# Multi-scale pooling moved out of the projection on GpSimd and into the output projection on VectorE, tile by tile

## The chip, the cores and the metric

The kernel runs on one core of a Trainium2 chip. A core has a matrix engine (TensorE, PE in the profile), a vector engine (VectorE, DVE), an engine for activations (ScalarE, ACT), a general engine (GpSimd, POOL) and one that mostly issues transfers (SyncE, SP). Each works through its instructions in the order in which they are written, and waits on semaphores where another engine or a transfer has to be done first. Transfers between the main memory (HBM) and the core's own memory (SBUF) run on 16 DMA engines. PE writes its results into PSUM, which VectorE and ScalarE read. The metric is the device time of one execution in microseconds.

## What is computed

One encoder layer over two groups of tokens, 1024 and 2048 long, with shared weights of width 1024. The half of it that matters here is the mixer: a projection of the normed input gives attention latents and 512 pooling channels `u`; attention and pooling are joined and go through one output projection.

```python
POOL_WINDOWS = (2, 4, 8, 16)          # one per group of 128 channels
def multiscale_pool(u, w_pool, pool_scale):
    ...
    for g, w in enumerate(POOL_WINDOWS):
        lo = jnp.clip(t - w // 2, 0, s)
        hi = jnp.clip(t + (w - w // 2), 0, s)
        ...
        means.append((cs_g[:, hi] - cs_g[:, lo]) / count)
    d = (mean - ug.astype(jnp.float32)).astype(u.dtype)
    y = jnp.einsum('bsgc,gcd->bsgd', d, w_pool).reshape(b, s, D_POOL)
    return y * pool_scale

def encoder_layer(...):
    h = rmsnorm(x) * (1 + sc1) + sh1
    c_q, c_kv, k_pe, u = jnp.split(h @ w_in, ...)
    att = latent_attention(c_q, c_kv, k_pe, ...)
    pool = multiscale_pool(u, w_pool, pool_scale)
    x = x + g1 * (jnp.concatenate([att, pool], axis=-1) @ w_out)
    h = rmsnorm(x) * (1 + sc2) + sh2
    return x + g2 * expert_choice_ffn(h, ...)
```

So each token's pooled value is the mean of `u` over a window of 2, 4, 8 or 16 tokens around it, cut at the ends of its group, minus `u` itself. The weights `w_pool` and `pool_scale` are folded into the output weights by the attention stage and play no part below.

## The kernel before

Six stages follow one another, each with a block of its own: `in_proj` (to about 430 us), `latent_proj` (to 645), `attention` for either group (to 1655), `out_proj` (to 1985), `selection` and `experts`. Results between stages lie in HBM scratch tensors with names in `s_`. Products are made of three passes of fp32r halves (`..h` high, `..l` low), so every operand is split: ScalarE writes the high half, VectorE subtracts it for the low half.

**`in_proj`** works on 24 tiles of 128 tokens in pairs and stores, among others, the pooling channels as `s_ut`, 4 groups of 128 channels by 3072 tokens, and the latents as `s_ct`.

**`latent_proj`** goes over 6 blocks of 512 tokens. A block is a list ORDER of 16 PSUM results: keys, queries, values and the rotary pairs r and t. PE makes them, ScalarE and VectorE split them (L955, L1009; rotary L990, L996, L947, L999), SP stores them (L872). Into this list, four times a block, the 24 jobs of the pooling are set: a job is one group of 128 channels over 512 tokens. SP loads it with 8 tokens on either side (`fetch`, L830), GpSimd doubles the window by adding a row to itself shifted (L794, the last step L792) and does the ends of a group with their own counts (L800, L803), VectorE scales and subtracts `u` (`difference`, L969), SP stores it to `s_diff` (`store_diff`, L837). The places are numbers in ORDER (POINTS), the same on SP and VectorE; two buffers `prj_u` and `prj_diff` alternate. SP's queue is one line: a job's store waits in front of the stores of the block's other results.

**`out_proj`** goes over 12 blocks of two tiles u = 0, 1. For block r:

- SP loads `mix[:, u]`, its lower half from `s_att` (L1628) and its upper half from `s_diff` (L1633), and the softmax denominators `rden` (L1631); then the residual input `x` (L1641), which for tile u waits until the previous block's `x1` of that tile is added. Since the queue is one line, the loads of `mix` for block r + 1 stand behind the `x` load for tile 1 of block r, and so behind the addition of `x1` for tile 1 of block r - 1.
- GpSimd multiplies the attention half by `rden` (`scale`, L1652) and adds `x1 = gated + x` (L1662). Its order is scale(r, 1), x1(r, 0), scale(r + 1, 0), x1(r, 1).
- ScalarE writes the high half of `mix` (`mix_high`, L1726), VectorE the low half (`mix_low`, L1800).
- PE multiplies (L1703 to L1705), behind tile 0 it transposes the previous block's `xn` (L1679), behind tile 1 it makes the router's logits (L1690).
- VectorE multiplies the result by the gate (`gated`, L1779); ScalarE squares `x1` for the norm (L1749, L1756), VectorE scales it to `xn` (L1787, L1793), and ScalarE's queue stores `x1` and `xn` (L1754, L1731).

VectorE's order in a block is the hand-written one that the change touches:

```python
def body(r, g, before, last=False):
    mix_low(r, 1, before is None)
    for u in range(2):
        dve.wait_ge(o_ready, 2 * r + u + 1)
        ...  # gated[:, u]
        if u == 0:
            if not last:
                mix_low(r + 1, 0, False)
    ...  # logits, reciprocal, xn
```

Blocks 0, 1, 4 and 11 are written out, 2 and 3 and 5 to 10 run in loops.

Of the kernel before, what the change touches and what calls it, by code (L numbers as in the profile page):

```python
# [30 lines left out]
P = 128  # L31
# [21 lines left out]
QUADS, QUAD = 4, 32  # L53

# [45 lines left out]
def in_proj(nc, w, keep):  # L100
# [17 lines left out]
    with ExitStack() as ctx:  # L118
# [25 lines left out]
        eps = m.sb("eps", [P, 1])  # L144
        t_ps = [m.ps(f"t_ps{i}") for i in range(2)]
# [19 lines left out]
        eps_set = m.sem("eps_set")  # L165
        x_squared = m.sem("x_squared")
# [37 lines left out]
        def _(sp):  # L204
# [38 lines left out]
            sp.dma_start(rope[:], w["k_rope"].rearrange("t p a c -> p t a c")).then_inc(rope_loaded, 16)  # L243
            for n in range(TILES):
# [8 lines left out]
                sp.dma_start(w["s_ut"][n % TB * UG:(n % TB + 1) * UG, :, b * T:(b + 1) * T].rearrange("g p t -> p g t"),  # L253
# [6 lines left out]
            sp.wait_ge(gates_stored, 64)  # L260
            for i in range(2):
# [384 lines left out]
def latent_proj(nc, w, keep):  # L646
# [10 lines left out]
    PAD = max(WINDOWS) // 2  # L657
    SPAN = BANK
    JOBS = [(g, c, o) for g in (1, 0) for c in range(len(WINDOWS)) for o in range(0, SEQS[g], SPAN)]
# [6 lines left out]
    JOBS_PER = len(JOBS) // NB  # L666
    POINTS = [PER * (i + 1) // JOBS_PER - 2 for i in range(JOBS_PER)]
    SIMPLE = [i for i, (kind, _) in enumerate(ORDER) if kind in "kqv"]
    SLOT = {"q": 0, "r": NQ, "k": NQ + RT, "v": NQ + RT + KT}
    with ExitStack() as ctx:  # L670
# [14 lines left out]
        u = m.sb("u", [P, 2, SPAN + 2 * PAD])  # L685
        sums = m.sb("sums", [P, 2, SPAN + 2 * PAD])
        diff = m.sb("diff", [P, 2, SPAN])
        edge = m.sb("edge", [P, len(WINDOWS), 2 * PAD])
        ends = m.sb("ends", [P, 2 * PAD])
# [16 lines left out]
        edge_in = m.sem("edge_in")  # L706
# [3 lines left out]
        total_ready = m.sem("total_ready")  # L710
        ends_ready = m.sem("ends_ready")
        pads_set = m.sem("pads_set")
        u_in = [m.sem(f"u_in{i}") for i in range(2)]
        summed = m.sem("summed")
        diff_ready = m.sem("diff_ready")
        diff_stored = [m.sem(f"diff_stored{i}") for i in range(2)]
        block = ctx.enter_context(nc.Block())

        def ends_of(n):
            g, _, o = JOBS[n]  # L720
            return o == 0, o + SPAN == SEQS[g]
# [39 lines left out]
        def _(pool):  # L761
            m.clear_last(pool)
            step = sequence(summed)
            pads = sequence(pads_set)

            def set_pads(n):

# [8 lines left out]
            for n in range(2):  # L776
                set_pads(n)
# [1834 lines left out]
```

## Time and profile before

| | us |
|---|---|
| median of three runs | 3834.94 |
| lowest and highest | 3832.25, 3835.29 |
| the profiled execution, device time | 3837.06 |
| its span in the trace | 3835.3 |
| PE busy | 3552.2 (93%) |
| DVE busy | 2026.7 (53%) |
| ACT busy | 1879.4 (49%) |
| POOL busy | 1271.3 (33%) |
| mean DMA rate | 141 GB/s |

The busy shares are sums over all stages, and stages have different limits. A stage is read from a window over it (busy time of each engine, granted clock of TensorE as a share of its full 2.4 GHz, share of the DMA engines) and from the timeline of single engines, where a row gives the start, the duration, what it does, and in brackets how long the engine sat idle before and what ended that wait. Starts are microseconds from the start of the span.

### The profile page before, as it was taken

The page shows a single profiled execution, that of the slowest core. Times are in us where ns is not written, and L with a number is a line of the kernel's source. Part 1 is how long each engine was busy: PE and PEld are TensorE (multiplying, and loading weights), DVE is VectorE, ACT ScalarE, POOL GpSimd, SP SyncE. Part 2 cuts the span into 40 slices and gives each one's busy share as a digit, 9 for nine tenths or more (in the row PEclk, how much of TensorE's full clock was granted, in tenths as well). Part 3 has the DMA queues.
Part 4 walks back from the last instruction along what each step waited for, and adds up shares of the span by engine and source line. Part 5 has one row for each costly group of instructions (what it writes and reads, how often), then busy time and mean ns, then how long its engine had stood idle before and what let it go on. Part 6 is the DMA issues. An engine that isn't in the chain of part 4 may idle for free. (4 is left out here: it accounts for less than half of the span.)

```text
span 3835.3 us, 54529 instructions
## 1 busy us (share of the span) xinstructions
PE 3552.2 (93%) x19090; PEld 3085.7 (80%) x19090; DVE 2026.7 (53%) x3177; ACT 1879.4 (49%) x3261; POOL 1271.3 (33%) x1006
## 2 busy tenths in 40 slices
PE   8999798998999999979973999999999999999993
PEld 5999676676777777757762999999999999999992
DVE  3333345787888888822237644444444444444444
ACT  4444223886889899933320343444434344343433
POOL 1111045886999899932320000000000000000000
PEclk8999898998999999989985999999999999999996
DMA  7445699630222222046641445445454444545447
GB/s 245 159 159 94 207 378 330 117 76 21 56 51 45 46 45 50 11 131 195 194 149 44 133 145 163 153 153 162 144 164 143 146 140 150 164 143 164 152 122 279
DMA packets 368694, 539.12 MB, mean 141 GB/s; under 512 B 39618, under 2 KB 257010, under 8 KB 365566
## 3 DMA queue, kind: packets, MB, share of 16 engines
q1 hardware_dynamic: 340356, 448.80, 38.4%
q0 software_dynamic: 13824, 50.34, 5.4%
q10 hardware_dynamic: 14336, 37.77, 2.5%
q8 instruction: 93, 1.52, 0.2%
q14 instruction: 85, 0.70, 0.1%
HBM read 394.27 MB, written 142.48 MB: 140 GB/s over the span
## 5 line engine op out<-in xcount | busy, mean ns | idle before, releaser
L1535 POOL TENSOR_TENSOR att_pr<-att_e,att_pr 128x512 fp32r<-128x512 f32 x640 | 815.8, 1299 | 138.8 <-ACT att_pr L1388 129.7
L2250 POOL DMA_INDIRECT s_x<-moe_ye,moe_to_add x48 | 92.9, 1935 | 1438.3 <-DVE moe_ye L2471 1429.1
L1453 DVE TENSOR_REDUCE att_mx<-att_m_ps 128x1 f32<-128x512 f32 x640 | 423.4, 682 | 68.7 <-PE att_m_ps L1266 60.6
L2409 DVE TENSOR_TENSOR keep_wl<-keep_raw,keep_wh 128x1024 fp32r<-128x1024 f32 x380 | 440.1, 1221 | 33.6 <-ACT keep_wh L2339 33.5
L2339 ACT ACTIVATE keep_wh<-keep_raw 128x1024 fp32r<-128x1024 f32 x380 | 370.0, 1045 | 123.1 <-PE moe_d_ps L2316 123.1
L1382 ACT ACTIVATE att_e<-att_s_ps 128x512 f32<-128x512 f32 x640 | 378.4, 591 | 67.8 <-PE att_s_ps L1293 36.8
L1388 ACT ACTIVATE att_pr<-att_e 128x512 fp32r<-128x512 f32 x640 | 402.7, 629 | 17.6 <-issue 2.2
L2366 ACT ACTIVATE moe_silu<-moe_a_ps 128x384 f32<-128x384 f32 x128 | 62.8, 491 | 653.3 <-PE moe_u_ps L2289 653.3
L1475 DVE TENSOR_TENSOR att_acc_ps<-att_acc_ps,att_e 128x512 f32<-128x512 f32 x544 | 374.9, 689 | 12.9 <-ACT att_e L1382 6.7
L2447 DVE TENSOR_TENSOR moe_hf<-moe_u_ps,moe_silu 128x384 f32<-128x384 f32 x128 | 71.4, 558 | 544.4 <-ACT moe_silu L2366 544.4
L2287 PE MATMUL moe_a_ps<-moe_xh,keep_wh 128*128 128x384 f32 x1024 | 345.7, 338 | 2.1 <-DVE moe_xl L2417 2.1
L2288 PE MATMUL moe_a_ps<-moe_xl,keep_wh 128*128 128x384 f32 x1024 | 345.1, 337 | 0.0
L2289 PE MATMUL moe_a_ps<-moe_xh,keep_wl 128*128 128x384 f32 x1024 | 344.9, 337 | 0.0
L2289 PE MATMUL moe_u_ps<-moe_xh,keep_wl 128*128 128x384 f32 x1024 | 344.4, 336 | 0.0
L2288 PE MATMUL moe_u_ps<-moe_xl,keep_wh 128*128 128x384 f32 x1024 | 344.2, 336 | 0.0
L2287 PE MATMUL moe_u_ps<-moe_xh,keep_wh 128*128 128x384 f32 x1024 | 344.2, 336 | 0.0
L1307 PE MATMUL att_o_ps<-att_pr,keep_ahead 128*128 128x512 f32 x1024 | 323.6, 397 | 2.5 <-POOL att_pr L1535 2.5
L2314 PE MATMUL moe_d_ps<-keep_wh,moe_hh 128*128 128x512 f32 x768 | 309.1, 402 | 4.9 <-DVE moe_ye L2471 3.0
L2316 PE MATMUL moe_d_ps<-keep_wh,moe_hl 128*128 128x512 f32 x768 | 302.8, 394 | 0.0
L2315 PE MATMUL moe_d_ps<-keep_wl,moe_hh 128*128 128x512 f32 x768 | 300.3, 391 | 0.0
L1307 PEld LDWEIGHTS att_o_ps<-att_pr,keep_ahead 128*128 128x128 f32 x1024 | 193.2, 190 | 48.8 <-POOL att_pr L1535 5.1
L1291 PE MATMUL att_s_ps<-keep_ahead 97*128 97x512 f32 x544 | 223.7, 411 | 4.0 <-issue 2.5
(284 smaller groups left out, 7702.1 us busy)
## 6 DMA issues: line engine op xcount, KB each, us to landing
keep_raw<-w_gate SPq DMA_DIRECT2D x64, 1024.0 KB, 5.1
keep_raw<-w_up SPq DMA_DIRECT2D x64, 1024.0 KB, 7.5
keep_raw<-w_down SPq DMA_DIRECT2D x64, 1024.0 KB, 6.7
inp_raw<-w_ada SPq DMA_DIRECT2D x48, 512.0 KB, 6.1
s_ct<-inp_ct SPq DMA_DIRECT2D x24, 640.0 KB, 3.1
prj_ct<-s_ct SPq DMA_DIRECT2D x6, 2560.0 KB, 12.5
s_kn<-prj_out SPq DMA_DIRECT2D x24, 512.0 KB, 9.1
s_qn<-prj_out SPq DMA_DIRECT2D x24, 512.0 KB, 9.2
```

Of the source, the lines that this page charges most:

```text
L1307: mm = nc.tensor.matmul(o_ps[b % 2][:, :], v[h][:, kt, :], pr[:, s % RING, a, :], start=(kt == 0 and a == 0), stop=(kt == NT - 1 and a == 1))
L1382: nc.scalar.activation(e[:, s % RING, :], s_ps[s % 2][:, :], ACT.Exp, scale=SCALE).then_inc(exp_done, 1)
L1388: nc.scalar.activation(pr[:, s % RING, 0, :], e[:, s % RING, :], ACT.Copy).then_inc(hi_done, 1)
L1453: nc.vector.tensor_reduce(mx[:, u % CB, u // CB:u // CB + 1], m_ps[u % MB][:, :], AX, ALU.max).then_inc(max_part, 1)
L1475: step = nc.vector.tensor_tensor(acc_ps[:, :], acc_ps[:, :], e[:, s % RING, :], ALU.add)
L1535: nc.gpsimd.tensor_tensor(pr[:, s % RING, 1, :], e[:, s % RING, :], pr[:, s % RING, 0, :].bitcast(F32), ALU.subtract).then_inc(lo_done, 1)
L2287: nc.tensor.matmul(out, hi, xh[:, k, :], start=(k == 0), stop=False)
L2288: nc.tensor.matmul(out, hi, xl[:, k, :], start=False, stop=False)
L2289: mm = nc.tensor.matmul(out, lo, xh[:, k, :], start=False, stop=(k == KD - 1))
L2314: nc.tensor.matmul(out, h_hi, wh[:, c % 2, k, :], start=(k == 0), stop=False)
L2339: nc.scalar.activation(wh[:, s, part, :], raw[:, s, part, :], ACT.Copy).then_inc(w_hi_done, 1)
L2409: nc.vector.tensor_tensor(wl[:, s, part, :], raw[:, s, part, :], wh[:, s, part, :].bitcast(F32), ALU.subtract).then_inc(w_lo_done, 1)
```

## The change

- `in_proj` stores `u` into an `s_ut` that has room for 8 tokens of zeros at either end of both groups (`HALO`), and writes those zeros once: a memset on GpSimd, a wait on SP and three small stores ahead of the stores of the tiles.
- `latent_proj` loses the pooling altogether: GpSimd's part, VectorE's `difference`, SP's `fetch` and `store_diff`, and `s_diff`.
- `out_proj` loads for every tile, where it loaded `s_diff`, 144 tokens of `s_ut` (`ut`), and VectorE pools them in nine instructions (`pooled`) into the upper half of `mix`. A table `inverse` with one over the count of every token, for a first, an inner and a last tile of a group, is loaded once. `mix_high` waits for `diff_done`, and so does SP before it loads over `ut`.
- The next block's two poolings stand on VectorE behind `mix_low(r, 1)` and behind the first gate. Blocks 0 to 4, 10 and 11 are written out now.

```diff
 # in_proj
+            sp.wait_ge(zeros_set, 1)
+            for at, size in ((0, HALO), (STARTS[1] + HALO, 2 * HALO), (TOKENS + 3 * HALO, HALO)):
+                sp.dma_start(w["s_ut"][:, :, at:at + size].rearrange("g p t -> p g t"), zeros[:, :, 0:size]
+                             ).then_inc(halo_stored, 16)
...
+                at = b * T + HALO * (1 + 2 * group(b))
+                sp.dma_start(w["s_ut"][n % TB * UG:(n % TB + 1) * UG, :, at:at + T].rearrange("g p t -> p g t"),
...
+            nc.gpsimd.memset(zeros[:], 0.0).then_inc(zeros_set, 1)
 # latent_proj, in SP's and VectorE's loops over ORDER; GpSimd's loop over JOBS goes as a whole
-                    if at in POINTS:
-                        n = JOBS_PER * b + POINTS.index(at)
-                        store_diff(n)
-                        if n + 2 < len(JOBS):
-                            fetch(n + 2)
...
-                    if n in POINTS:
-                        difference(JOBS_PER * b + POINTS.index(n))
 # out_proj, SP
-                    sp.dma_start(mix[:, u, KA:KD], w["s_diff"][:, :, bass.ds(r * 2 * P + u * P, P)]
-                                 .rearrange("c p t -> p c t")).then_inc(mix_in[u], 16)
+                    if before is not None:
+                        sp.wait_ge(diff_done, 2 * r - (1 - u))
+                    at = r * 2 * P + u * P + 2 * HALO * g
+                    sp.dma_start(ut[:, u], w["s_ut"][:, :, bass.ds(at, SPAN)].rearrange("c p t -> p c t")
+                                 ).then_inc(ut_in[u], 16)
+                    if before is None and u == 0:
+                        sp.dma_start(inverse[:].rearrange("p a c t -> p (a c t)"),
+                                     w["k_inverse"].partition_broadcast(P)).then_inc(inverse_in, 16)
 # GpSimd
-                pool.wait_ge(mix_in[u], 32 * r + 32)
+                pool.wait_ge(mix_in[u], 16 * r + 16)
 # ScalarE
             def mix_high(r, u, first):
                 act.wait_ge(att_scaled, 2 * r + u + 1)
+                act.wait_ge(diff_done, 2 * r + u + 1)
 # VectorE
+            def pooled(r, u):
+                n = 2 * r + u
...
+                dve.wait_ge(ut_in[u], 16 * r + 16)
+                if not isinstance(n, int) or n:
+                    dve.wait_ge(diff_done, n)
+                src = ut[:, u]
+                for level in range(KA):
+                    reach = 1 << level >> 1
+                    lo, hi = 2 * reach + (level == 0), SPAN - 2 * reach + (level > 0)
+                    back, ahead = (reach, reach) if level else (1, 0)
+                    nc.vector.tensor_tensor(total[:, level], src[:, 0, HALO - back:HALO + P - back],
+                                            src[:, 0, HALO + ahead:HALO + P + ahead], ALU.add).then_inc(total_done, 1)
+                    if level < KA - 1:
+                        dst = sums[level]
+                        nc.vector.tensor_tensor(dst[:, :, lo:hi], src[:, 1:, lo - back:hi - back],
+                                                src[:, 1:, lo + ahead:hi + ahead], ALU.add).then_inc(level_done[level], 1)
+                        dve.wait_ge(level_done[level], n + 1)
+                        src = dst
+                dve.wait_ge(total_done, KA * n + KA)
+                nc.vector.tensor_tensor(total[:], total[:], inverse[:, edge], ALU.mult).then_inc(mean_done, 1)
+                dve.wait_ge(mean_done, n + 1)
+                nc.vector.tensor_tensor(mix[:, u, KA:KD], total[:], ut[:, u, :, HALO:HALO + P],
+                                        ALU.subtract).then_inc(diff_done, 1)
+
             def body(r, g, before, last=False):
                 mix_low(r, 1, before is None)
+                if not last:
+                    pooled(r + 1, 0)
                 for u in range(2):
                     dve.wait_ge(o_ready, 2 * r + u + 1)
...
                     if u == 0:
                         if not last:
+                            pooled(r + 1, 1)
                             mix_low(r + 1, 0, False)
```

VectorE in a block of the output projection before, from `xn` of one block to `xn` of the next (`outp_ml` is the low half, `outp_gated` the gate):

```order
L1793 TENSOR_SCALAR outp_xn<-outp_x,outp_ms 128x1024 x2
L1800 TENSOR_TENSOR outp_ml<-outp_mix,outp_mh 128x1024
L1779 TENSOR_TENSOR outp_gated<-outp_o_ps,outp_g 128x1024
L1800 TENSOR_TENSOR outp_ml<-outp_mix,outp_mh 128x1024
L1779 TENSOR_TENSOR outp_gated<-outp_o_ps,outp_g 128x1024
L1770 COPY keep_logits<-outp_l_ps 128x256
L1787 RECIPROCAL outp_ms<-outp_ms 128x2
```

The same place now, from the low half to the first gate; the nine instructions of a pooling read `outp_ut` and end in `outp_mix`:

```order
L1753 TENSOR_TENSOR outp_ml<-outp_mix,outp_mh 128x1024
L1709 TENSOR_TENSOR outp_total<-outp_ut 128x128
L1713 TENSOR_TENSOR outp_sums<-outp_ut 128x3x143
L1709 TENSOR_TENSOR outp_total<-outp_sums 128x128
L1713 TENSOR_TENSOR outp_sums<-outp_sums 128x2x141
L1709 TENSOR_TENSOR outp_total<-outp_sums 128x128
L1713 TENSOR_TENSOR outp_sums<-outp_sums 128x137
L1709 TENSOR_TENSOR outp_total<-outp_sums 128x128
L1718 TENSOR_TENSOR outp_total<-outp_total,outp_inverse 128x512
L1720 TENSOR_TENSOR outp_mix<-outp_total,outp_ut 128x512
L1731 TENSOR_TENSOR outp_gated<-outp_o_ps,outp_g 128x1024
```

A pooling now stands between the low half and the first gate, and a second one, the same nine rows, between that gate and the next `outp_ml`.

SP at the border of two blocks before, the loads of `x` for one block and those of the next block's first tile behind them:

```order
L1641 DMA outp_x<-x_prompt 128x1024 x2
L1628 DMA outp_mix<-s_att 128x4x128
L1631 DMA outp_rden<-s_rden 64x4x128 x2
L1633 DMA outp_mix<-s_diff 128x4x128
L1628 DMA outp_mix<-s_att 128x4x128
```

And now:

```order
L1562 DMA outp_x<-x_prompt 128x1024 x2
L1543 DMA outp_mix<-s_att 128x4x128
L1546 DMA outp_rden<-s_rden 64x4x128 x2
L1551 DMA outp_ut<-s_ut 128x4x144
L1543 DMA outp_mix<-s_att 128x4x128
```

The load of `outp_ut` has the place that the load of `s_diff` had: fourth of its tile, behind the loads of `x`.

## Rows read from the trace of the kernel before

**Rows 1.** the page, part 1: busy us (share of the span) xinstructions

```profile
PE 3552.2 (93%) x19090; PEld 3085.7 (80%) x19090; DVE 2026.7 (53%) x3177; ACT 1879.4 (49%) x3261; POOL 1271.3 (33%) x1006
```

**Rows 2.** windows: length; busy PE, PEld, DVE, ACT, POOL; clock, DMA share, GB/s

```profile
560.00:580.00 20.00, 9.92 (x40) 7.86 (x39) 4.82 (x8) 2.73 (x6) 6.29 (x7) 0.77 1.04 360
...
1800.00:1850.00 50.00, 49.52 (x256) 39.60 (x255) 13.49 (x16) 16.61 (x30) 14.22 (x8) 1.00 0.62 189
```

**Rows 3.** timeline of PE in the projection: start, us, what, [idle before <-releaser]

```profile
577.89 0.79 PE L921 MATMUL prj_ps<-prj_wv,prj_ct 128*128 128x512 f32 x1 [10.08 <-DVE prj_out L1009]
...
631.06 0.39 PE L923 MATMUL prj_ps<-prj_ct,prj_wq 128*128 128x512 f32 x1
645.75 4.73 PE L1266 MATMUL att_m_ps<-keep_ahead 96*128 96x512 f32 x8 [14.30 <-PEq L670]
```

**Rows 4.** timelines of POOL and DVE in the projection

```profile
571.84 1.06 POOL L794 TENSOR_TENSOR prj_sums<-prj_u 128x527 f32<-128x527 f32 x1 [14.59 <-DMA prj_u<-s_ut]
...
576.54 0.69 DVE L969 SCALAR_TENSOR_TENSOR prj_diff<-prj_diff,prj_u 128x512 f32<-128x512 f32 x1 [14.81 <-POOL prj_diff L792]
...
638.09 0.68 DVE L969 SCALAR_TENSOR_TENSOR prj_diff<-prj_diff,prj_u 128x504 f32<-128x504 f32 x1 [2.90 <-POOL prj_diff L792]
```

**Rows 5.** DMA issues, 400 to 720 us: count, KB, median us to landing

```profile
s_diff<-prj_diff SPq DMA_DIRECT2D x24, 256.0 KB, 7.4
prj_u<-s_ut SPq DMA_DIRECT2D x16, 260.0 KB, 7.9
...
prj_u<-s_ut SPq DMA_DIRECT2D x8, 264.0 KB, 9.3
```

**Rows 6.** timeline of POOL in the output projection

```profile
1797.43 2.40 POOL L1662 TENSOR_TENSOR outp_x<-outp_gated,outp_x 128x1024 f32<-128x1024 f32 x1 [7.01 <-DVE outp_gated L1779]
...
1809.81 2.39 POOL L1662 TENSOR_TENSOR outp_x<-outp_gated,outp_x 128x1024 f32<-128x1024 f32 x1 [8.72 <-DVE outp_gated L1779]
1813.70 1.29 POOL L1652 TENSOR_TENSOR outp_mix<-outp_mix,outp_rden 128x512 f32<-128x512 f32 x1 [1.50 <-DMA outp_mix<-s_diff]
1822.66 2.40 POOL L1662 TENSOR_TENSOR outp_x<-outp_gated,outp_x 128x1024 f32<-128x1024 f32 x1 [7.67 <-DVE outp_gated L1779]
```

**Rows 7.** timeline of SP in the output projection

```profile
1804.54 1.25 SPq L1633 DMA_DIRECT2D outp_mix<-s_diff  x1
```

**Rows 8.** line L1633, all 24 loads of s_diff

```profile
DMA to landing us min/median/max: 6.2/8.7/10.8
```

**Rows 9.** timelines of DVE and ACT in the output projection

```profile
1808.33 1.23 DVE L1779 TENSOR_TENSOR outp_gated<-outp_o_ps,outp_g 128x1024 f32<-128x1024 f32 x1 [4.21 <-PE outp_o_ps L1705]
1816.28 1.23 DVE L1800 TENSOR_TENSOR outp_ml<-outp_mix,outp_mh 128x1024 fp32r<-128x1024 f32 x1 [6.72 <-ACT outp_mh L1726]
1821.35 1.23 DVE L1779 TENSOR_TENSOR outp_gated<-outp_o_ps,outp_g 128x1024 f32<-128x1024 f32 x1 [3.85 <-PE outp_o_ps L1705]
...
1815.10 1.06 ACT L1726 ACTIVATE outp_mh<-outp_mix 128x1024 fp32r<-128x1024 f32 x1 [1.58 <-POOL outp_mix L1652]
```

**Rows 10.** lines L996, L487: ns min/median/max, first and last start, forms

```profile
L996 DVE TENSOR_TENSOR prj_qf<-prj_prod x12: 692/694/1510, 470.0 to 640.1; 128x512 f32<-128x512 f32 x12
...
L487 DVE TENSOR_TENSOR inp_ct<-inp_c_ps,inp_ct x24: 280/281/281, 68.3 to 428.0; 128x128 fp32r<-128x128 f32 x24
```

**Rows 11.** timelines, projection: a GpSimd addition beside a DVE one

```profile
626.73 1.06 POOL L794 TENSOR_TENSOR prj_sums<-prj_u 128x527 f32<-128x527 f32 x1 [0.59 <-DMA prj_u<-s_ut]
...
626.85 1.50 DVE L996 TENSOR_TENSOR prj_qf<-prj_prod 128x512 f32<-128x512 f32 x1
```

**Rows 12.** POOL at the start of out_proj, and line L1622, two broadcasts

```profile
1668.60 1.26 POOL L1652 TENSOR_TENSOR outp_mix<-outp_mix,outp_rden 128x512 f32<-128x512 f32 x1 [15.32 <-DMA outp_mix<-s_diff]
...
DMA to landing us min/median/max: 6.5/6.8/7.1
```

**Rows 13.** timeline of POOL, additions of second tiles, blocks 0 and 10

```profile
1697.76 2.39 POOL L1662 TENSOR_TENSOR outp_x<-outp_gated,outp_x 128x1024 f32<-128x1024 f32 x1 [7.24 <-DVE outp_gated L1779]
...
1948.79 2.40 POOL L1662 TENSOR_TENSOR outp_x<-outp_gated,outp_x 128x1024 f32<-128x1024 f32 x1 [7.67 <-DVE outp_gated L1779]
```

More of the change, by code:

```diff
@@ L762, in _ @@
             m.clear_last(pool)
-            step = sequence(summed)
-            pads = sequence(pads_set)
-            def set_pads(n):
-                first, last = ends_of(n)
-                if first:
-                    pads(nc.gpsimd.memset(u[:, n % 2, 0:PAD], 0.0))
-                if last:
-                    pads(nc.gpsimd.memset(u[:, n % 2, PAD + SPAN:], 0.0))
             for i in range(2):
                 nc.gpsimd.memset(rows[:, i, :].bitcast(F32), float(i)).then_inc(rows_set, 1)
-            for n in range(2):
-                set_pads(n)
@@ L886, in _ @@
             sp.wait_ge(ahead_in, 16 * (HEAD_LOADS - 1))
-            for i in range(2):
-                sp.wait_ge(diff_stored[i], 16 * len(JOBS) // 2)
         @block.tensor
@@ L962, in _ @@
                                                ALU.subtract).then_inc(w_lo_done, 1)
-            def difference(n):
-                c = JOBS[n][1]
-                first, last = ends_of(n)
-                a, b = PAD * first, SPAN - PAD * last
-                dve.wait_ge(total_ready, n + 1)
-                nc.vector.scalar_tensor_tensor(diff[:, n % 2, a:b], diff[:, n % 2, a:b], 1.0 / WINDOWS[c],
-                                               u[:, n % 2, PAD + a:PAD + b], ALU.mult, ALU.subtract).then_inc(diff_ready, 1)
             dve.wait_ge(tabs_in, 2 * 16 * (P // ROPE))
@@ L1567, in out_proj @@
         mix = m.sb("mix", [P, 2, KD, P])
+        ut = m.sb("ut", [P, 2, KA, SPAN])
+        sums = [m.sb(f"sums{i}", [P, KA - 1 - i, SPAN]) for i in range(KA - 1)]
+        total = m.sb("total", [P, KA, P])
+        inverse = m.sb("inverse", [P, 3, KA, P])
         rden = m.sb("rden", [P, 2, KA, P])
@@ L1587, in out_proj @@
         att_scaled = m.sem("att_scaled")
+        ut_in = [m.sem(f"ut_in{i}") for i in range(2)]
+        inverse_in = m.sem("inverse_in")
+        level_done = [m.sem(f"level_done{i}") for i in range(KA - 1)]
+        total_done = m.sem("total_done")
+        mean_done = m.sem("mean_done")
+        diff_done = m.sem("diff_done")
         mix_hi_done = m.sem("mix_hi_done")
@@ L1608, in over_blocks @@
             body(0, 0, None)
-            body(1, 0, 0)
-            with eng.Fori(2, SPLIT) as r:
-                body(r, 0, 0)
-            body(SPLIT, 1, 0)
-            with eng.Fori(SPLIT + 1, BLOCKS - 1) as r:
+            for r in range(1, SPLIT + 1):
+                body(r, int(r == SPLIT), 0)
+            with eng.Fori(SPLIT + 1, BLOCKS - 2) as r:
                 body(r, 1, 1)
+            body(BLOCKS - 2, 1, 1)
             body(BLOCKS - 1, 1, 1, last=True)
@@ L2548 @@
     "s_rows": [2, max(SEQS)],
-    "s_diff": [DP // P, P, TOKENS],
     "s_x": [TOKENS, D],
```

94 lines of the change are left out of this document (17 added, 77 removed).

## The prediction

> **What bounds the kernel now.** I read the busy shares first: TensorE (PE) has 93% of the span, VectorE (DVE) 53% [rows 1]. Such a share says nothing of a stage, so next came the windows over the two stages that the change touches.
>
> In the projection (`latent_proj`, 430 to 645 us) the DMA engines are full: share 1.04 in a window in which PE idles half the time at a granted clock of 0.77 [rows 2]. PE waits there 10.08 us for a DVE copy [rows 3]; DVE has waited 14.81 us for GpSimd (POOL), and POOL 14.59 us for a load of `prj_u` [rows 4]. So one late pooling load holds three engines, each of which does its work in written order. The same chain closes the stage: PE's last product starts at 631.06, the next stage's first at 645.75 after 14.30 us idle [rows 3], because DVE's last pooling subtraction, at 638.09, is queued ahead of its last rotary chain [rows 4].
>
> In the output projection (`out_proj`, 1660 to 1985 us) PE is busy 49.52 of 50 us at full clock while DVE works only 13.49 [rows 2]. The block time is PE's: the addition L1662 of the second tile goes from 1697.76 to 1948.79 in ten blocks, 25.1 us each [rows 13]. What matters is how much time the other engines have beside PE.
>
> **What the change removes.** 24 stores of `s_diff` and 24 loads of `prj_u` leave the full DMA stretch, 24x256 + 16x260 + 8x264 KB or 12.7 MB [rows 5]; at the 360 GB/s of that window [rows 2] about 35 us of transfer. Both waits go with them. Terms: PE's stall 10.1 us [rows 3]; the slow clock behind it, 1.6 us (the 0.77 of 20 us is 4.6 us short of full, and most of that lies inside the stall) [rows 2]; the tail, where DVE could go on when PE ends at about 631.5 but is held until 638.09 + 0.69, some 7.2 us [rows 3, 4]; and the two first loads, 0.5 MB, that stand ahead of the query weights on SP's queue, 1.3 us. Sum **-20 us**. With 16% fewer bytes the stores should no longer back up, so I see nothing else late there. The least is the stall alone with a slow landing behind it, -10; the most, -23.
>
> The input projection gains a memset, three small halo stores and one SP wait on GpSimd. They are issued early in that stage, and nothing reads the halo before the output projection: priced at nothing. If their landing (the nearest row is 6.5 to 7.1 us for a broadcast [rows 12]) delayed the loads behind them without cover, it would cost up to 7 us; a gain has no source.
>
> **What it adds to DVE.** One pooling is nine additions, products and differences: four of 128 elements, one each of 429, 282 and 137, two of 512. The rows give 0.28 us for 128 elements and 0.69 for 512 [rows 10], so 0.144 us each and 1.07 ns an element: 1.30 + 2.55 = 3.85 us. Six waits on its own results come on top; between nothing and 1.1 us, I take 4.2 us. Two a block are 8.4 us on an engine that idles 18 of 25. By sums it fits.
>
> **Where it stands is what decides.** The pooling of the next block's first tile stands behind `mix_low(r, 1)` and *ahead of* the gate of this block's first tile. Its input is loaded by SP as the fourth DMA of a batch, and that batch stands behind the loads of `x`, the second of which waits until GpSimd has added the previous block's second tile. The trace shows that date for the transfer in the same place, `s_diff`: the addition ends at 1797.43 + 2.40 = 1799.83, SP issues `s_diff` at 1804.54 [rows 7], and it is there at 1813.70, when GpSimd's scaling, idle until then, starts [rows 6]: 13.9 us. From issue to landing the 24 took 6.2 to 10.8, so 10.9 to 15.5 us behind the addition [rows 8]. Before, this was harmless: the scaling that waits stands behind the first gate, and had 1.50 us to lose [rows 6]. Now DVE itself waits, and the gate, which started at 1808.33 or 8.5 us behind the addition [rows 9], cannot start before 13.9 + 4.2 = 18.1.
>
> That closes a loop without PE in it: addition of the second tile, load, pooling, first gate, second pooling, low half, second gate, addition. Its pieces:
> - load: 13.9 (10.9 to 15.5)
> - pooling: 4.2 (3.85 to 5.0)
> - start of the first gate to start of `mix_low(r+1, 0)`: without mutual hindrance 1808.33 to the addition's end at 1812.20 is 3.87; scaling to `mix_high`, 1813.70 to 1815.10, is 1.40; to `mix_low` at 1816.28 another 1.18 [rows 6, 9]: 6.45, beside which DVE's gate and second pooling, 1.2 + 4.2, fit. But this pooling now runs against GpSimd's addition and scaling, 2.39 + 1.29 us. Such a pair is in the projection: a DVE addition with both inputs in SBUF takes 694 ns in the median and 1510 at most [rows 10], and it was the 1510 that started 0.12 us behind a GpSimd addition [rows 11]. If DVE waits out all of GpSimd's time, 1.2 + 4.2 + 3.7 = 9.1. I take 8.5, since a DVE addition or two gets in first.
> - `mix_low` 1.2, second gate to addition 1.3 (1821.35 to 1822.66), addition 2.4 [rows 6, 9]
>
> Sum 31.5 us against 25.1. PE has its work done in time and then waits 6 us for `mix_low` in each block; its clock may fall there, but with 6 us to spare that costs nothing. Ten rounds: **+64 us** (28.5 to 34 us a block: +34 to +89).
>
> On this hindrance the Trainium skill has a rule ("SBUF — State Buffer", Who interferes with whom): a VectorE instruction with two SBUF inputs and a GpSimd one that reads SBUF exclude each other for a whole instruction. By it the loop is 32.1 us; by the median row it is 29.5. No run here shows the two together in this stage.
>
> The start of the stage: GpSimd's first scaling starts at 1668.60, when the first batch has landed [rows 12]; now the first `mix_high` needs a pooling of 4.2 us, which runs beside the scaling of 1.3, and the table of inverses, a broadcast behind it (such a one lands in 6.5 to 7.1 us [rows 12]), about 1.2 us later: **+4 us** (2.5 to 6). The last block has no poolings and costs nothing more. Unrolled blocks change no work.
>
> **Sum.** The profiled execution took 3837.06 us, 2.1 above the median of the three. 3837.1 - 20 + 4 + 64 = 3885, or **3883 us** against the median: slower by 1.3%.
>
> **Rivals.** (1) *The poolings hide and the projection's gain stays*: -20 + 4, 3819 us, faster. For it speaks DVE's idle time [rows 2]; it decides if the load is there 25.1 - 4.2 - 8.5 - 4.9 = 7.5 us behind the addition or less, and no landing before was under 10.9 [rows 8]. (2) *No hindrance between DVE and GpSimd*: 29.5 us a block, +44, 3863. (3) *The projection stays DMA-bound*, so that the removed bytes only shorten queues and the 20 us shrink to 3: 3900. The full share speaks for it, PE's idle time against it. (4) *Half-way*: loads land near 10.9 because the batch has less to share with, hindrance is slight: about 26.5 us a block, +14, with the -20 within 0.2% of before.
>
> The Trainium skill ("GPSIMD Engine Reference", Engine selection) sends elementwise additions to VectorE, GpSimd being about twice as slow; that is the reason of rival 1. As a price per instruction the rows agree (0.69 us here, 1.06 there [rows 10, 11]); what it leaves out is where the instruction waits.
>
> **Chances.** Forecast 0.70, rival 2 0.10, rival 3 0.04, rival 4 0.04, rival 1 0.12. About 0.2%, 7.7 us, is what a measurement of this kernel can tell from no change: faster 0.12, same 0.04, slower 0.84. The range from 3848 to 3915 takes the loop from 28.5 to 34 us with the smaller terms beside it, rivals 2 and 3 included, and leaves out rivals 1 and 4 and the outermost bounds.
>
> **What would show it.** Right: in the profile after, the gap of 10 us in the projection is gone and its end comes some 20 us earlier; in the output projection DVE waits for a DMA of `outp_ut` ahead of its pooling, PE waits some 6 us a block for `outp_ml`, and the additions of second tiles stand about 31.5 us apart. Wrong: PE still 99% busy there and 25 us a block (rival 1); pooling instructions under GpSimd's addition as short as alone (rival 2); PE's gap in the projection still there (rival 3).

## The result, and the profile after

Over four runs each the changed kernel took 3880.67 us in the median (3875.95 to 3884.70) and the kernel before 3833.89 (3832.25 to 3835.29): a ratio of 1.0122, interval 1.0110 to 1.0134. The forecast was 3883. The profiled execution of after took 3875.95 us (span 3874.2), 38.9 more in span than the one of before. It is the fastest of its four; the medians differ by 46.8.

The page's first part, in the columns of [rows 1], shows nothing alarming: VectorE (DVE) is busy for 2132.7 us, 106 more, GpSimd (POOL) for 1194.0, 77 less, and the share of TensorE (PE) falls by one point to 92%.

The two windows of [rows 2], again. In the projection PE now works 20.00 of 20 us, at a DMA share that is still 1.04. In the output projection it works 44.76 of 50 us instead of 49.52, and its granted clock, 1.00 before, is 0.93.

```profile
560.00:580.00 20.00, 20.00 (x90) 16.57 (x89) 10.19 (x15) 6.78 (x13) 0.00 (x0) 1.00 1.04 414
1800.00:1850.00 50.00, 44.76 (x207) 35.41 (x206) 20.32 (x33) 14.69 (x27) 11.13 (x6) 0.93 0.57 178
```

PE at the end of the projection: its last product starts at 611.83, and the attention's first stands 6.50 us idle behind it, against 14.30 in [rows 3]. From the first product of the projection to the first of the attention it was 444.77 to 645.75 before, 200.98 us, and is 439.42 to 618.71, 179.29 us: **21.7 us gained**. Both first products, the kernel before's (L921) ahead of the changed one's, and then the end:

```profile
444.77 0.79 PE L921 MATMUL prj_ps<-prj_ct,prj_wk 128*128 128x512 f32 x1 [18.37 <-DMA prj_ct<-s_ct]
...
439.42 0.79 PE L837 MATMUL prj_ps<-prj_ct,prj_wk 128*128 128x512 f32 x1 [18.21 <-DMA prj_ct<-s_ct]
...
611.83 0.39 PE L839 MATMUL prj_ps<-prj_ct,prj_wq 128*128 128x512 f32 x1
618.71 3.54 PE L1171 MATMUL att_m_ps<-keep_ahead 96*128 96x512 f32 x6 [6.50 <-PEq L676]
```

In the output projection DVE now waits for the load of `ut`, and PE for the low half. In the kernel before DVE waited for no such load, and PE for the low half only once, 17.6 us at the start of the stage. The waits from 1600 to 2060 us, as total, times and longest (the 23.1 is the start here):

```profile
DVE outp_total L1709 <- DMA outp_ut<-s_ut: 99.8, 11, 11.2
...
PE outp_o_ps L1624 <- DVE outp_ml L1753: 62.0, 11, 23.1
```

The additions of second tiles, against [rows 13]: (1987.66 - 1678.20) / 10 = **30.95 us a block**, 25.1 before, 58.4 us lost in ten blocks. (Before, the first of the ten distances is 23.99 us and the others 25.23; the latter is meant below by the steady part.)

```profile
1678.20 2.39 POOL L1583 TENSOR_TENSOR outp_x<-outp_gated,outp_x 128x1024 f32<-128x1024 f32 x1 [7.14 <-DVE outp_gated L1731]
...
1987.66 2.36 POOL L1583 TENSOR_TENSOR outp_x<-outp_gated,outp_x 128x1024 f32<-128x1024 f32 x1 [5.18 <-DVE outp_gated L1731]
```

One block of it, from one addition of a second tile to the next. The rows are ordered by engine, on POOL, SP, DVE, POOL, DVE and POOL; compare [rows 6, 7, 9]:

```profile
1769.51 2.36 POOL L1583 TENSOR_TENSOR outp_x<-outp_gated,outp_x 128x1024 f32<-128x1024 f32 x1 [5.18 <-DVE outp_gated L1731]
...
1776.33 1.25 SPq L1551 DMA_DIRECT2D outp_ut<-s_ut  x1
...
1785.69 0.29 DVE L1709 TENSOR_TENSOR outp_total<-outp_ut 128x128 f32<-128x128 f32 x1 [9.52 <-DMA outp_ut<-s_ut]
...
1789.42 1.22 DVE L1731 TENSOR_TENSOR outp_gated<-outp_o_ps,outp_g 128x1024 f32<-128x1024 f32 x1
...
1790.72 2.39 POOL L1583 TENSOR_TENSOR outp_x<-outp_gated,outp_x 128x1024 f32<-128x1024 f32 x1 [17.61 <-DVE outp_gated L1731]
1793.07 1.66 POOL L1573 TENSOR_TENSOR outp_mix<-outp_mix,outp_rden 128x512 f32<-128x512 f32 x1
...
1790.76 2.82 DVE L1713 TENSOR_TENSOR outp_sums<-outp_ut 128x429 f32<-128x429 f32 x1
1793.61 1.27 DVE L1709 TENSOR_TENSOR outp_total<-outp_sums 128x128 f32<-128x128 f32 x1
...
1797.48 1.22 DVE L1753 TENSOR_TENSOR outp_ml<-outp_mix,outp_mh 128x1024 fp32r<-128x1024 f32 x1
1798.61 1.22 DVE L1731 TENSOR_TENSOR outp_gated<-outp_o_ps,outp_g 128x1024 f32<-128x1024 f32 x1
...
1799.91 2.37 POOL L1583 TENSOR_TENSOR outp_x<-outp_gated,outp_x 128x1024 f32<-128x1024 f32 x1 [5.18 <-DVE outp_gated L1731]
```

The addition ends at 1769.51 + 2.36 = 1771.87. SP issues `ut` at 1776.33, it is there at 1785.69, where DVE starts the first pooling; the gate follows at 1789.42. Now DVE's second pooling meets POOL's addition and scaling: the 429-element addition that takes 0.60 us alone takes 2.82, the next 1.27 instead of 0.29, and POOL's scaling 1.66 instead of 1.30, the median before. The low half starts at 1797.48, the second gate at 1798.61, the addition at 1799.91. The next lines give the shortest, median and longest of the 429-element additions in ns, and the time from issue to landing of all 24 loads of `ut`:

```profile
L1713 DVE TENSOR_TENSOR outp_sums<-outp_ut x24: 597/602/2827, 1645.1 to 1978.5; 128x429 f32<-128x429 f32 x24
...
DMA to landing us min/median/max: 5.4/8.4/11.5
```

The start of the stage, from the first load at 1634.00 to PE's first product at 1652.12, 18.1 us, where it was 1660.31 to 1672.33, 12.0 us, before (the first two rows are the kernel before's):

```profile
1660.31 0.40 SPq L1628 DMA_DIRECT2D outp_mix<-s_att  x1
...
1672.33 0.79 PE L1703 MATMUL outp_o_ps<-keep_wo_h,outp_mh 128*128 128x512 f32 x1 [17.59 <-DVE outp_ml L1800]
...
1634.00 0.40 SPq L1543 DMA_DIRECT2D outp_mix<-s_att  x1
...
1636.47 0.50 SPq L1554 DMA_DIRECT2D outp_inverse<-k_inverse  x1
...
1644.87 0.29 DVE L1709 TENSOR_TENSOR outp_total<-outp_ut 128x128 f32<-128x128 f32 x1 [10.42 <-DMA outp_inverse<-k_inverse]
...
1647.99 1.63 DVE L1720 TENSOR_TENSOR outp_mix<-outp_total,outp_ut 128x512 f32<-128x512 f32 x1
...
1647.37 1.71 POOL L1573 TENSOR_TENSOR outp_mix<-outp_mix,outp_rden 128x512 f32<-128x512 f32 x1 [4.18 <-DMA outp_rden<-s_rden]
...
1652.12 0.79 PE L1624 MATMUL outp_o_ps<-keep_wo_h,outp_mh 128*128 128x512 f32 x1 [23.11 <-DVE outp_ml L1753]
```

The table of inverses, issued at 1636.47, lands 8.4 us later and lets the first pooling begin; its last subtraction takes 1.63 us beside POOL's second scaling. From the first load to the addition of block 0's second tile it was 37.45 us and is 44.20.

**The account of the profiled pair.** Input projection -5.3 (first product of the projection at 444.77 and 439.42), projection -21.7, attention +0.7, start of the output projection +6.8, ten blocks +58.4, last block +2.0 (27.19 against 25.23); sum +40.9 of +38.9. The remaining -2 lies behind the stage and isn't placed. Why the last block is longer wasn't looked into.

The -5.3 can't be put down to the change. In the 13 profiles of kernels with the changed first stage (those of the experiments below among them), the granted clock over the first 50 us goes from 0.74 to 0.93 and the projection's first product starts from 438.5 to 448.4, in the changed kernel itself at 439.4 and 443.1 in two profiles. The one profile of the kernel before, with 0.73 and 444.77, lies within those starts. Without the -5.3 the placed terms give 46.2 us, and 44.2 with the unplaced -2; the medians differ by 46.8.

### The profile page after: what moved, and what is told of

Read it like the earlier page. It is cut to its first block and busy times, and to the rows that moved or that the text cites. A ratio compares the mean times of both kernels' runs of the same rounds, so it can differ in the third digit from the quotient of the medians.

```text
span 3874.2 us, 54356 instructions
## 1 busy us (share of the span) xinstructions
PE 3565.7 (92%) x19090; PEld 3096.1 (80%) x19090; DVE 2132.7 (55%) x3369; ACT 1883.1 (49%) x3261; POOL 1194.0 (31%) x899
## 6 DMA issues: line engine op xcount, KB each, us to landing
s_kn<-prj_out SPq DMA_DIRECT2D x24, 512.0 KB, 10.1
```

## The experiments

The theory: a loop without TensorE sets the block, from the second tile's addition over SP's queue, the landing of `ut`, DVE's pooling ahead of the gate, the gate, the second pooling beside GpSimd's work, the low half and the second gate back to the addition. The rivals: VectorE's added work as such; the added traffic. The kernel before took 3844.88, 3837.88, 3840.48 and 3845.95 us on the four occasions below, so whole times are compared as ratios on one occasion, and stages by their profiles. The kernel before was profiled on none of the four. The whole times expected for a to d were reckoned from 3834 us; held against the kernel before on their own occasion, all four took 5 to 13 us less than the middle of what was expected, and a's stages don't show where. So the blocks are the better test there.

### a: the projection's part alone

```diff
 def out_proj: as in the kernel before, but
-    mix[:, u, KA:KD] <- s_diff[..., r * 2 * P + u * P]
+    mix[:, u, KA:KD] <- s_ut[..., r * 2 * P + u * P + 2 * HALO * g + HALO]
```

> Leaves out the pooling: the pooling is gone from the projection, as in the changed kernel, and the output projection is that of the kernel before, except that the upper half of the mix is loaded from the unpooled values. So it holds the gain of the projection alone. Loop theory: the projection gives back 21 us (its end gap 14.3 to 6.5, and 13 to 14 us inside it), the output projection keeps 25.1 us a block, so about 3813 us (3806 to 3820). Rival, the gain was only 3 us because the stage is bound by its transfers: 3831. Rival, the loss of the changed kernel lies outside the output projection (halo stores, a later stage): over 3835.

Measured: 3817.39 us, ratio 0.9929 (0.9911 to 0.9948), or 20 to 34 us. The stages of its profile, set against the profile of before, give 20 of the 27 in the middle of that; the other 7 aren't placed. The projection took 179.8 us, first product to first product, against 201.0 before; the blocks are back at (1927.66 - 1676.53) / 10 = 25.11 us. The projection's gain is real, and all of the loss is in the output projection.

```profile
1676.53 2.39 POOL L1567 TENSOR_TENSOR outp_x<-outp_gated,outp_x 128x1024 f32<-128x1024 f32 x1 [7.23 <-DVE outp_gated L1684]
...
1927.66 2.40 POOL L1567 TENSOR_TENSOR outp_x<-outp_gated,outp_x 128x1024 f32<-128x1024 f32 x1 [7.35 <-DVE outp_gated L1684]
```

### b: the same work, the load earlier

```diff
 SP, body(r): the batch for block r without ut, then
     x load of tile 0
+    for v in range(2): wait diff_done >= 2r + 1 + v; ut[:, v] <- s_ut of block r + 1
     x load of tile 1 (waits for the previous block's second addition)
```

> The changed kernel with one edit on SP's queue: the two loads of ut for the next block are issued between the two loads of x instead of behind the second one, so they no longer wait for the second tile's addition. VectorE's order, its work and the bytes are those of the changed kernel. Loop theory: ut is there by about 3 us behind the addition instead of 13.8, the pooling ends before TensorE has the first tile's sum, and the additions of second tiles stand 25.1 to 25.6 us apart: 3834 - 21 + 7 + 0 to 5, or 3820 to 3825 us. Rival, VectorE's own work and its hindrance by GpSimd set the block: still 29.5 to 31 us a block, 3864 to 3880. Rival, the bytes of ut load the DMA engines: no change, 3880.

Measured: 3826.56 us, ratio 0.9952 (0.9936 to 0.9968), faster than the kernel before. DVE's instructions and the bytes are those of the changed kernel; the blocks fell to (1939.30 - 1683.39) / 10 = 25.59 us. DVE pools from 1791.71 and waits at the gate for PE, not for a DMA. Its second pooling is still held up beside POOL (the 429-element addition takes 2.82 us in this block too), but the block doesn't wait for it:

```profile
1683.39 2.40 POOL L1589 TENSOR_TENSOR outp_x<-outp_gated,outp_x 128x1024 f32<-128x1024 f32 x1 [7.14 <-DVE outp_gated L1737]
...
1939.30 2.40 POOL L1589 TENSOR_TENSOR outp_x<-outp_gated,outp_x 128x1024 f32<-128x1024 f32 x1 [8.62 <-DVE outp_gated L1737]
```

```profile
1791.71 0.29 DVE L1715 TENSOR_TENSOR outp_total<-outp_ut 128x128 f32<-128x128 f32 x1
...
1796.22 1.23 DVE L1737 TENSOR_TENSOR outp_gated<-outp_o_ps,outp_g 128x1024 f32<-128x1024 f32 x1 [0.70 <-PE outp_o_ps L1632]
```

So neither the work nor the traffic alone makes the 31 us: the date of the load does.

### c: the same load, the work later

```diff
 DVE, body(r):
     mix_low(r, 1)
-    pooled(r + 1, 0)
     gate of tile 0
-    pooled(r + 1, 1)
+    pooled(r + 1, 0)
     mix_low(r + 1, 0)
     gate of tile 1
+    pooled(r + 1, 1)
```

> The changed kernel with one edit on VectorE: the pooling of the next block's first tile stands behind the first gate, that of its second tile behind the second gate. SP's queue is that of the changed kernel, so ut still lands about 13.8 us behind the second tile's addition. Loop theory: the gate no longer waits for the load; load 13.8, pooling 3.7, mix_high 1.2, mix_low 1.2 give the next low half 20 us behind the addition, just before TensorE asks for it (8.5 + 12.5 = 21), so 25.1 to 26 us a block and 3820 to 3830 us. Rival, VectorE's work and hindrance: the same amount stands on VectorE, 29.5 to 31 us a block, 3864 to 3880.

Measured: 3830.99 us, ratio 0.9957 (0.9944 to 0.9971), 25.60 us a block. SP's queue is untouched and DVE still waits for `ut`, 3.34 us in this block, but behind the gate, and with the low half at 1784.67 it is ready before the gate that follows it:

```profile
1774.88 1.22 DVE L1729 TENSOR_TENSOR outp_gated<-outp_o_ps,outp_g 128x1024 f32<-128x1024 f32 x1 [1.18 <-PE outp_o_ps L1626]
1779.44 0.53 DVE L1709 TENSOR_TENSOR outp_total<-outp_ut 128x128 f32<-128x128 f32 x1 [3.34 <-DMA outp_ut<-s_ut]
...
1784.67 1.23 DVE L1751 TENSOR_TENSOR outp_ml<-outp_mix,outp_mh 128x1024 fp32r<-128x1024 f32 x1 [1.17 <-ACT outp_mh L1648]
1788.24 1.22 DVE L1729 TENSOR_TENSOR outp_gated<-outp_o_ps,outp_g 128x1024 f32<-128x1024 f32 x1 [2.34 <-PE outp_o_ps L1626]
```

The loop was cut at its other end, with the same result.

### d: a smaller dose

```diff
 SP, body(r), for u in range(2):
+    ut[:, u] <- s_ut
     mix[:, u, 0:KA] <- s_att
     rden[:, u] <- s_rden (two)
-    ut[:, u] <- s_ut
```

> The changed kernel with ut as the first DMA of each tile's batch on SP instead of the fourth; it still stands behind the second load of x, and so behind the second tile's addition. A smaller dose of the same cause. Loop theory: issue some 4 us earlier, so the loop is some 4 us shorter, 27 us a block (26 to 28.5), 3840 us (3830 to 3856). Rival, the landing is set by the traffic of the batch and not by the issue: 30 to 31 us a block, 3870 to 3880. Rival, VectorE's work: no change, 3880.

Measured: 3837.57 us, ratio 0.9980 (0.9969 to 0.9990), (1950.33 - 1687.74) / 10 = 26.26 us a block (first two rows). In one block the addition ends at 1790.77 + 2.40 = 1793.17, `ut` is issued at 1794.31 and there at 1800.57, 7.4 us behind the addition where it was 13.8:

```profile
1687.74 2.41 POOL L1583 TENSOR_TENSOR outp_x<-outp_gated,outp_x 128x1024 f32<-128x1024 f32 x1 [7.17 <-DVE outp_gated L1731]
...
1950.33 2.40 POOL L1583 TENSOR_TENSOR outp_x<-outp_gated,outp_x 128x1024 f32<-128x1024 f32 x1 [5.18 <-DVE outp_gated L1731]
```

```profile
1790.77 2.40 POOL L1583 TENSOR_TENSOR outp_x<-outp_gated,outp_x 128x1024 f32<-128x1024 f32 x1 [5.82 <-DVE outp_gated L1731]
...
1794.31 0.38 SPq L1546 DMA_DIRECT2D outp_ut<-s_ut  x1
...
1800.57 0.29 DVE L1709 TENSOR_TENSOR outp_total<-outp_ut 128x128 f32<-128x128 f32 x1 [3.11 <-DMA outp_ut<-s_ut]
```

Over blocks 0 to 9, worked out in the same way, the load is there 9.0 us behind the addition (7.4 to 11.0), and in the changed kernel 14.4 (13.6 to 15.5): 3.0 us of it from the earlier issue, where I had expected 4, and 2.4 from a shorter landing, which I had not expected. That would make the loop 25.6 us, as long as PE's own block of 25.7; the blocks with late landings lie above it, hence 26.3. In the four blocks whose load came 9.7 us or more behind the addition, the distance to the next addition is that time and another 16.6 to 16.7 us, as in the changed kernel (30.95 - 14.4). One move on the queue undid four fifths of the loss (4.7 of 5.9 us a block). The block lies in the range expected; the whole time is 7 us under the kernel before's, where 6 over it had been expected (3840 against 3834).

### e: more GpSimd time beside the second pooling

```diff
 POOL, body(r):
     x1 addition of tile 0
     scaling of block r + 1, tile 0
+    spare[:, 1] = spare[:, 0] + spare[:, 0]     (1024 elements, read by nobody)
```

> The changed kernel with one more GpSimd addition a block, 1024 elements of a spare tile that nobody reads, right behind the scaling of the next block's first tile, where GpSimd has stood idle for 5 us. It doubles the time for which VectorE's second pooling runs beside a GpSimd addition. Loop theory with hindrance: VectorE waits out that addition too, 2.4 us more between the first gate and the low half, so 33.3 us a block (32.5 to 34) instead of 30.95, and 3900 to 3907 us. Rival, the long VectorE rows beside GpSimd are an accident of the trace and the block is set by the load alone: no change, 30 to 31 us a block.

Measured: 3897.01 us in one run, 32.56 us a block. POOL has nothing to do there otherwise, and nobody waits for the spare tile, yet DVE's 282-element addition, 0.45 us alone, takes 2.14:

```profile
1804.16 1.94 POOL L1594 TENSOR_TENSOR outp_spare<-outp_spare 128x1024 f32<-128x1024 f32 x1
...
1804.28 2.14 DVE L1724 TENSOR_TENSOR outp_sums<-outp_sums 128x282 f32<-128x282 f32 x1
```

30.95 + 2.14 - 0.45 = 32.64. Without the time to the landing of the load, which varies, the rest of the loop is 18.3 us in each of the ten blocks, where it is 16.6 in the changed kernel: 1.7 more, and 2.14 - 0.45 is 1.69. The added addition took 1.94 us, not the 2.4 that I had taken from the other, which has two different inputs; so the block lies at the lower end of the expected range, and the time 3 us under the 3900 expected. The hindrance is a cause by itself.

### g, h, j, m: the slower product

b and c left a question: PE is busy throughout in both, and still a block takes 25.70 us in the steady part, not 25.23. PE's products start every 0.232 us instead of every 0.227.

```diff
 g: b, with ut, sums, total, inverse allocated at the end of the stage
 h: a, with these tiles allocated where the changed kernel has them, unused
 j: h, with 128 bytes more of unused tile behind them
 m: h, with the unused tiles behind mh and ml instead of ahead of rden
```

> The kernel with the early loads (b), with the four new groups of tiles (ut, sums, total, inverse) allocated last in the stage instead of ahead of rden, mh and ml, so that the old tiles lie at the addresses that they had before. Open since b and c: TensorE, busy all the time in both, starts a product every 0.232 us there and every 0.227 us in the kernel before and in a, which makes 25.70 us of 25.23 a block. If the addresses do it: 0.227 and 25.2 us a block, 5 to 6 us faster than b. If VectorE's pooling or the added traffic does it: 0.232 and 25.7 us a block, as b.

> The kernel with the projection's part alone (a, no pooling at all), with the new tiles allocated where the changed kernel has them but never used. The other half of the question of g. If the addresses do it: a product every 0.232 us and 25.7 us a block, some 5 us over a. If VectorE's pooling or its traffic does it: 0.227 us and 25.2 us a block, as a.

> The kernel h (projection's part alone, no pooling, unused tiles where the changed kernel has its new ones) with one more unused tile of 128 bytes behind them. The new tiles take 16256 bytes of each partition, 128 short of 64 x 256; with the spare tile the old ones lie exactly 16384 bytes above the addresses that they had before. If the slower product of h (0.232 us, 25.70 a block) comes from how rden, mh and ml lie against a step of 256 bytes or more: 0.227 us and 25.2 us a block. If it comes from where they lie at all (how far up): 25.7 us a block, as h.

> The kernel h with the same unused tiles placed behind mh and ml instead of ahead of rden: rden, mh and ml, the two that TensorE reads as stationary operands of the products in question, are back at the addresses that they had before, and all later tiles (x, gated, x1, xn, junk, h2 and the small ones) stay shifted by 16256 bytes. If the address of mh and ml makes the products slow: 0.227 us and 25.2 us a block. If that of a later tile does it: 0.232 us and 25.7 us a block, as h.

Measured, block distances: g 25.11, h 25.59, j 25.11, m 25.12 us (g 3819.51 us, ratio 0.9959, 0.9944 to 0.9974; h, j and m one run each, 3822.19, 3815.45 and 3823.63, of which m's projection began 5.6 us later than h's). The second and the last of the 48 products of one tile, in h and then in j; the 46 steps between them take 10.68 us in h, 0.232 each, and 10.46 in j, 0.227 each:

```profile
1789.37 0.39 PE L1613 MATMUL outp_o_ps<-keep_wo_l,outp_mh 128*128 128x512 f32 x1
...
1800.05 0.40 PE L1614 MATMUL outp_o_ps<-keep_wo_h,outp_ml 128*128 128x512 f32 x1
```

```profile
1787.86 0.39 PE L1614 MATMUL outp_o_ps<-keep_wo_l,outp_mh 128*128 128x512 f32 x1
...
1798.32 0.39 PE L1615 MATMUL outp_o_ps<-keep_wo_h,outp_ml 128*128 128x512 f32 x1
```

No instruction differs between h, j and m, only where the tiles lie, and no data are read from the unused tiles. The three ran on different chips, but each of the three chips shows both spacings: 0.232 to 0.234 in b, h and l, 0.227 to 0.228 in m, g and k on the same chips. It is the address of `rden`, `mh` or `ml` that costs 2% of PE's time here: 16256 bytes up is slow, 16384 is not. That it is `mh` and `ml`, which PE reads as the stationary operand, is the likely reading; the three were moved together. g's ratio doesn't show its 5 us over b, since the two were measured on different occasions and each interval is some 12 us wide; the block distances do.

### k and l: the same move in the changed kernel

```diff
 k: the changed kernel, with ut, sums, total, inverse allocated at the end of the stage
 l: the changed kernel as it is
```

> The changed kernel with nothing but its new tiles allocated last. TensorE's products get their old length, 0.227 us. Loop theory: the loop has no TensorE in it, so the block stays at 30 to 31 us and the time at that of the changed kernel (within 5 us of it; the first block and the last, where TensorE does count, give at most 1 us). Rival, the slower products are part of the loss: 0.47 us a block less, 30.5 us, and 5 to 6 us less.

> The changed kernel as it is, on the chip of j and k, for the comparison with k: 30 to 31.5 us a block, 1.2% over the kernel before.

Measured: k 3886.08 us, ratio 1.0113 (1.0096 to 1.0130), 31.40 us a block; l 3888.89, 1.0121 (1.0102 to 1.0140), 31.02 us a block. No difference that can be told, although the products start every 0.227 us in k and every 0.233 in l: with PE outside the loop, faster products buy nothing. k's longer block is its loads', which are there 14.8 us behind the addition in the mean, and 14.4 in l. Subtract from each distance between two additions the time that its load took to be there, counted from the end of the first of them: what is left is 16.5 to 16.6 us in all 30 blocks of k, l and the changed kernel's first profile. That rest of the loop is the same with slow products and with fast ones.

### i: a version that beats both

```diff
 g, and in block 0:
 SP:  ut and inverse are the first loads, mix and rden follow
 DVE:
-    wait inverse_in ahead of pooled(0, 0)
+    wait inverse_in inside it, ahead of the product with the table
```

> g with the start of the output projection mended: in block 0 ut and the table of inverses are the first two loads instead of the fourth and fifth, and VectorE waits for the table only where it reads it, ahead of the seventh of nine instructions. Loop theory: the first low half comes 2.5 to 4 us sooner (TensorE's first product 14.5 to 15.5 us behind the stage's start instead of 18.1), the rest is g, so 2.5 to 4 us faster than g, and 20 to 25 us faster than the kernel before. Rival, the first scaling, whose loads are now behind, comes later and eats it: as g.

Measured: 3814.53 us, ratio 0.9945 (0.9931 to 0.9958), 5 us faster than g in the median on the same occasion, and 0.55% faster than the kernel before. The single runs of i and g overlap; it is the start of the stage that tells them apart. PE's first product stands at 1649.42 - 1636.87 = 12.6 us behind the stage's first load, where it is 19.7 in g, 18.1 in the changed kernel and 12.0 before the change:

```profile
1636.87 0.40 SPq L1541 DMA_DIRECT2D outp_ut<-s_ut  x1
...
1640.48 0.29 DVE L1715 TENSOR_TENSOR outp_total<-outp_ut 128x128 f32<-128x128 f32 x1 [3.16 <-DMA outp_ut<-s_ut]
...
1645.70 1.26 POOL L1579 TENSOR_TENSOR outp_mix<-outp_mix,outp_rden 128x512 f32<-128x512 f32 x1 [15.26 <-DMA outp_rden<-s_rden]
...
1649.42 0.79 PE L1630 MATMUL outp_o_ps<-keep_wo_h,outp_mh 128*128 128x512 f32 x1 [17.52 <-DVE outp_ml L1761]
```

It went further than expected, since the pooling (from 1640.48) is now over before the first scaling (1645.70) begins: the scaling, which does come later, ends the wait again, as in the kernel before. Blocks: 25.10 us. The start costs nothing any more (37.6 us to block 0's second addition, 44.6 in g, 37.45 before), and what is left is the projection's gain.

## Why the prediction was right

**Projection, -20: right.** -21.7 in the profiled pair and 179.6 to 181.4 us against 201.0 in all later profiles. Its terms came out one by one: the gap of 10.1 us is gone, with a second wait of 0.2 for the same copies; PE's busy time fell by 2.0 (168.75 to 166.73 us, the slow clock forecast at 1.6); its wait for the query weights fell by 1.6 (7.7 to 6.1, forecast 1.3); the end gap fell by 7.8 (7.2 forecast). Rival 3 took the full DMA share for a bound; after, PE works all 20 us of the window at the same 1.04, with 414 GB/s in place of 360. The full share said that queues were long, not that PE waited for them.

**Start, +4: too small, +6.8**, and outside the 2.5 to 6 given. Two of its rows were taken too low: the table landed in 8.4 us, not 6.5 to 7.1 [rows 12], behind four other loads; and the last subtraction, 1.63 us instead of 0.69, met POOL's second scaling, which I had left out here while counting just that in the block. The slower products add 0.6.

**The loop, 31.5: right, piece by piece.** In the block shown: load 13.8 (13.9 forecast), pooling 3.73 (4.2), gate to low half 8.06 (8.5), low half to second gate 1.13 (1.2), gate to addition 1.30 (1.3), addition 2.36 (2.4). Sum 30.4. In the mean of ten blocks the load is there 14.4 us behind the addition, and with that and the other 16.6 the sum is the 30.95 measured. So the load was 0.5 too early in the forecast and the two poolings 0.9 too long, which partly cancels. The date of `s_diff`, which had the same place in the queue, gave the largest piece to within 0.5 us. In the pooling, the waits on its own results, for which I had allowed up to 1.1 us, cost nothing that shows: 3.73 us against 3.85 for the bare instructions.

**Hindrance between DVE and GpSimd: right.** 8.06 us is the gate, a pooling of 3.7, and 3.2 us of waiting out of POOL's 2.39 + 1.66. The Trainium skill's rule ("SBUF — State Buffer", Who interferes with whom), by which the two exclude each other for a whole instruction, agrees with these rows: 602 ns in the median and 2827 beside an addition of 2.39 us; in e 2.14 us behind one of 1.94. The loop stayed below the 32.1 us that it would give if all of POOL's time were waited out, since DVE's first short addition gets in ahead and POOL's scaling waits for DVE in its turn. Rival 2, 29.5 us without hindrance, is out. (As a price, the two rows that the prediction compares, 0.69 and 1.06 us, make GpSimd 1.5 times as slow and not twice; nothing in the sum hangs on it.)

**Rival 1, the poolings hide: out for the change as made, true once the load is early.** Its condition was a load at most 7.5 us behind the addition; in the changed kernel the load never came under 13.6. In b, where the load has landed by the time DVE comes to it, PE sets the block again (25.6 us).

**PE's wait of some 6 us: right in sum, wrong in kind.** It waits 62.0 - 23.1 = 38.9 us in ten blocks, 3.9 each. The rest of the 5.9 is slower work: in the ten blocks PE is busy for 268.19 us where it was 248.65, 2.0 more a block. Of these 0.5 are the address, and the other 1.5 are the clock: in the block shown, after 3.27 us idle and a few products more, the granted clock falls to 0.50 of full speed, the 1.2 GHz level, and is back at 1.00 by the second window (a row of PE's timeline, then two windows in the columns of [rows 2]):

```profile
1768.35 0.50 PE L1624 MATMUL outp_o_ps<-keep_wo_h,outp_mh 128*128 128x512 f32 x1 [3.27 <-DVE outp_ml L1753]
...
1769.80:1772.60 2.80, 2.80 (x8) 2.23 (x7) 0.00 (x0) 0.70 (x1) 2.80 (x2) 0.50 0.00 0
1774.00:1780.00 6.00, 6.00 (x27) 4.86 (x26) 2.17 (x3) 0.33 (x1) 0.00 (x0) 1.00 0.92 335
```

2.80 us at half speed lose 1.4, and over each of the ten blocks the clock is 0.92 to 0.95. All of it lies in PE's slack, as forecast; l and k, with and without the 0.5, show the same time.

**Sum.** 3883 forecast, 3880.67 measured; as a loss, 48 and 46.8. The loop was 5.6 too large and the projection's gain 1.7 too small; the start was 2.8 too small, and the last block and the attention, forecast at nothing, cost 2.0 and 0.7. That these nearly cancel is luck: the mechanism is the one forecast, the single terms are good to some 6 us and not to 2. The input projection's halo, priced at nothing with a bound of 7, is lost in a start that varies by 10 us among kernels with the same first stage.

## What to carry to other kernels

An engine that is idle 18 of 25 us can still lose time if an instruction that waits for a late load stands in its queue ahead of one on which everybody depends: follow each new wait back to the date at which its load can be issued, and look whether that date depends on the queued instruction's own successors. If it does, the loop can be cut at either end, by issuing the load earlier (b) or by placing the consumer behind the gate (c). Adding a tile moves all tiles behind it, so compare the spacing of TensorE's products before and after; here it was enough to allocate the new tiles last (g).

## What the runs showed of the hardware that was not expected

- The products of the output projection start every 0.232 us instead of 0.227 when `rden`, `mh` and `ml` lie 16256 bytes higher, at full granted clock and with nothing changed but where the tiles lie (h against a), and every 0.227 us again at 16384 (j): 25.70 against 25.23 us a block. Which of the three it is, and which step of the address counts, was not tried further.
- The same load of `ut` lands in 2.9 to 8.2 us, median 3.9, where it is issued between the loads of `x` (b, the line below), and in 5.4 to 11.5, median 8.4, as fourth of a batch. In front of its batch, the first tile's load landed 2.4 us faster than behind it (d, mean of ten).

```profile
DMA to landing us min/median/max: 2.9/3.9/8.2
```

- A GpSimd addition of a tile with itself took 1.94 us in all 11 blocks of e, one of two different tiles of the same size 2.39. The latter also writes over one of its inputs; which of the two makes the difference wasn't tried.
